# A mixer and two MLPs in split float32: x laid out twice, parameters as columns, TensorE's loops written out

## The reference

```python
u = rms_norm(h, mix_pre_gain)
p = u @ w_in                                     # 2048 x 5120
b_gate, c_gate, v_a, val_b, gate_b = split(p)
y_a = b_gate * causal_dwconv(c_gate * v_a, conv_a_w)          # 3 taps
g = causal_dwconv(val_b * sigmoid(gate_b), conv_b_w) + conv_b_bias   # 31 taps
y_b = silu(layer_norm(g, ln_b_gain, ln_b_bias))
h = h + rms_norm(concat(y_a, y_b) @ w_out, mix_post_gain)
m = rms_norm(h, mlp_pre_gain)
z = square(relu(m @ w_up)) @ w_down              # 2048 x 8192 and back
h = h + rms_norm(z, mlp_post_gain)
```

```python
proj = rmsnorm(h, g_mix) @ w_in_2                # q, k, v and three gates
merged = sum(sigmoid(gate_b) * (o_b @ w_branch_b) for b in range(3))
h = h + merged @ w_out_2
h = h + (silu(f @ w_gate) * (f @ w_up)) @ w_down_2   # f = rmsnorm(h, g_ffn)
```

## Time and profile before

| | us |
|---|---|
| median of 3 runs (2528.92 to 2530.01) | 2529.46 |
| the profiled execution's own time | 2525.66 |
| its span, first to last instruction | 2523.9 |

### The profile page before, as it was taken

The page is one execution under the profiler, slowest core; times in us unless marked ns, Lnnn a source line. Parts: engine busy times, 40 slices in busy tenths (PEclk is TensorE's granted clock), DMA queues, the critical chain, the costliest instruction groups (busy, mean ns, idle before and its releaser), DMA issues.

```text
span 2523.9 us, 30348 instructions
## 1 busy us (share of the span) xinstructions
PE 2489.8 (99%) x11139; PEld 2064.8 (82%) x11139; DVE 1455.9 (58%) x1552; ACT 1361.6 (54%) x1721; POOL 67.0 (3%) x78
## 2 busy tenths in 40 slices
PE   8999999999999999899999999999999999999999
PEld 7888878888788788788888888888888888888887
DVE  5888566555455455665566645545555555555554
ACT  5886566456455455454475544445555445544453
POOL 0110000000000000010100000000000000000000
PEclk9999999999999999999999999999999999999999
DMA  7897668677667676455555566665667666766665
GB/s 248 240 264 213 201 174 234 209 214 217 197 184 218 183 212 205 150 191 186 184 181 168 173 195 189 190 194 171 198 203 209 203 194 200 206 206 195 202 192 167
DMA packets 304214, 502.40 MB, mean 199 GB/s; under 512 B 70276, under 2 KB 70844, under 8 KB 303836
## 3 DMA queue, kind: packets, MB, share of 16 engines
q1 hardware_dynamic: 299372, 483.78, 62.9%
q0 software_dynamic: 4688, 16.93, 3.1%
q10 hardware_dynamic: 32, 0.01, 0.0%
HBM read 474.42 MB, written 4.47 MB: 190 GB/s over the span
## 4 chain that ended last, share of the span: by engine, by line
PE 98%; ACT 1%; DVE 1%; issue 0%; DMA 0%; POOL 0%; SPq 0%; ACTq 0%; DVEq 0%
PE acc L429 32%; PE acc L431 32%; PE acc L430 32%; PE tp L446 1%; PE po L615 0%; DVE w_lo L1074 0%; ACT w_hi L696 0%; PE sc L585 0%; DMA h<-x_dram 0%; ACT yb L846 0%; PE tp L603 0%; PE po L617 0%; ACT ev L703 0%; PE sc L446 0%; PE po L446 0%
## 5 line engine op out<-in xcount | busy, mean ns | idle before, releaser
L1074 DVE TENSOR_TENSOR w_lo<-raw,w_hi 128x1024 fp32r<-128x1024 f32 x888 | 1077.3, 1224 | 887.5 <-ACT w_hi L696 886.7
L696 ACT ACTIVATE w_hi<-raw 128x1024 fp32r<-128x1024 f32 x888 | 931.8, 1059 | 960.2 <-PE acc L431 933.7
L429 PE MATMUL acc<-w_lo,a_hi 128*128 128x512 f32 x2304 | 902.7, 392 | 9.8 <-issue 8.6
L431 PE MATMUL acc<-w_hi,a_lo 128*128 128x512 f32 x2304 | 898.0, 390 | 0.0
L430 PE MATMUL acc<-w_hi,a_hi 128*128 128x512 f32 x2304 | 897.7, 390 | 0.0
L430 PEld LDWEIGHTS acc<-w_hi,a_hi 128*128 128x128 f32 x2304 | 433.7, 188 | 96.0 <-issue 7.3
L429 PEld LDWEIGHTS acc<-w_lo,a_hi 128*128 128x128 f32 x2304 | 433.7, 188 | 92.9 <-issue 3.7
L431 PEld LDWEIGHTS acc<-w_hi,a_lo 128*128 128x128 f32 x2304 | 433.4, 188 | 90.6
L429 PE MATMUL acc<-w_lo,b_hi 128*128 128x512 f32 x1120 | 436.2, 389 | 0.3 <-DVE w_lo L1074 0.3
L431 PE MATMUL acc<-w_hi,b_lo 128*128 128x512 f32 x1120 | 435.7, 389 | 0.0
L430 PE MATMUL acc<-w_hi,b_hi 128*128 128x512 f32 x1120 | 435.7, 389 | 0.0
(11 more groups left out here) (171 smaller groups left out, 949.0 us busy)
## 6 DMA issues: line engine op xcount, KB each, us to landing
raw<-w_in_dram SPq DMA_DIRECT2D x272, 512.0 KB, 4.5
raw<-w_down_dram SPq DMA_DIRECT2D x216, 512.0 KB, 4.7
raw<-w_gu_dram SPq DMA_DIRECT2D x176, 512.0 KB, 4.4
raw<-w_up_dram SPq DMA_DIRECT2D x128, 512.0 KB, 3.9
raw<-w_out_dram SPq DMA_DIRECT2D x64, 512.0 KB, 4.6
raw<-w_branch_dram SPq DMA_DIRECT2D x32, 512.0 KB, 3.7
tap_sum<-tap_add POOLq DMA_DIRECT2D x20, 512.0 KB, 7.0
skew_dram<-line_dram POOLq DMA_DIRECT2D x12, 192.0 KB, 4.8
```

Of the source, the lines that this page charges most:

```text
L429: nc.tensor.matmul(out, xh, wl, start=s == 0 and k == 0, stop=False)
L431: mm = nc.tensor.matmul(out, xl, wh, start=False, stop=s == n - 1 and k == KS - 1)
L696: nc.scalar.activation(w_hi[:, ring], raw[:, ring], ACT.Copy).then_inc(hi_ready, 1)
L1074: nc.vector.tensor_tensor(w_lo[:, ring], raw[:, ring], w_hi[:, ring].bitcast(F32), ALU.subtract).then_inc(lo_ready, 1)
```

## The change

- The caller's program lays out two more inputs: `xT`, x with channels on partitions (128 x 16 x 256), and `cols`, all parameters per channel as columns (128 x 384). Both are made from the inputs by reordering alone.
- The first unit takes its activations from `xt`, loaded in eight pieces of two channel blocks (256 KB each), one behind each weight slot. ScalarE makes `a_hi` and VectorE `a_lo` from it directly, slot by slot. TensorE has no transposes in unit 0 and none of parameters; the product of the bias table moves behind unit 1.
- The rows of x are still needed, for the sums of squares and the residual. They are loaded in unit 1, one quarter behind each of its first four slots; ScalarE takes the squares while it prepares those slots.
- The other parameters, the tables and the identity are loaded behind unit 1's slots.
- TensorE's three loops become Python loops, so that its program has their bodies in full: 10785 rows of instructions for 8064. The loops of the other engines stay.

```diff
@@ -64,7 +63,7 @@
 G_FF3 = G_FF + 192
 G_DN3 = G_FF3 + 48
 G_END = G_DN3 + 24
-T_X, T_IN, T_N1, T_N2, T_QK, T_ATT, T_M, T_N3, T_FF = 0, 8, 20, 28, 36, 52, 68, 76, 84
+T_IN, T_N1, T_N2, T_QK, T_ATT, T_M, T_N3, T_FF = 0, 12, 20, 28, 44, 60, 68, 76
 S_X, S_YA, S_YB, S_N1, S_MLP, S_N2, S_O, S_M, S_N3, S_FF = 0, 8, 12, 16, 24, 56, 64, 80, 88, 96
 K_QK, K_ATT = 8, 24
 X_MLP, X_FF = 0, 16
@@ -100,7 +99,7 @@
         a_lo = at("a_lo", 64, [P, KT, S], F32R)
         b_hi = at("b_hi", 80, [P, KT, S], F32R)
         b_lo = at("b_lo", 96, [P, KT, S], F32R)
-        rows = at("rows", 112, [P, 4, P])
+        xt = at("xt", 80, [P, KT, S])
         onehot = at("onehot", 114, [32, LINE])
         lmask = at("lmask", 116, [H_SOFT, LINE])
         line = at("line", 118, [H_SOFT, LINE])
@@ -307,32 +307,28 @@
                     ).then_inc(planes_turned, 16)
-            sp.dma_start(ident[:, :], t["ident"]).then_inc(ident_in, 16)
-            for c in range(NCH):
-                sp.dma_start(h[:, :, c], x_v[:, :, c]).then_inc(x_in[c], 16)
-                load(c, None, w_in[:, ks(c), IN_COLS[0]:IN_COLS[0] + W])
-
-            small = ((16, "mlp_pre_gain", KT), (32, "g_mix_2", KT), (48, "g_ffn_2", KT),
-                     (64, "conv_b_bias", CT), (72, "ln_b_gain", CT), (80, "ln_b_bias", CT),
-                     (88, "conv_a_w", K_A * CT))
-            for r0, name, n in small:
-                src = t[name][0]
-                src = (src.rearrange("(c p) -> c p", p=P) if len(src.shape) == 1
-                       else src.rearrange("k (c p) -> (k c) p", p=P))
-                sp.dma_start(rows[r0:r0 + n, 0, :], src).then_inc(rows_in, 16)
-            taps = t["conv_b_w"][0].rearrange("k (c p) -> (k c) p", p=P)
-            for i in range(2):
-                sp.dma_start(rows[0:124, 1 + i, :], taps[124 * i:124 * (i + 1), :]).then_inc(rows_in, 16)
-            sp.dma_start(rows[0:H_SOFT, 3, :], t["q_gain_2"][0]).then_inc(rows_in, 16)
-            sp.dma_start(rows[H_SOFT:2 * H_SOFT, 3, :], t["k_gain_2"][0]).then_inc(rows_in, 16)
-            sp.dma_start(onehot[:, :], t["onehot"]).then_inc(line_in, 16)
-            sp.dma_start(lmask[:, :], t["lmask"]).then_inc(line_in, 16)
-            sp.dma_start(relb[:, :], t["rel_bias_2"]).then_inc(line_in, 16)
+            def load_xt(s):
+                sp.dma_start(xt[:, ks(s), :], t["xT"][:, ks(s), :]).then_inc(xt_in[s], 16)
+
+            for s in range(RING):
+                load(s, None, w_in[:, ks(s), IN_COLS[0]:IN_COLS[0] + W])
+                load_xt(s)
             for u in range(10):
                 for s in range(SPU):
                     g = G_IN + u * SPU + s
-                    if g >= RING:
-                        load(g, g, w_in[:, ks(s), IN_COLS[u]:IN_COLS[u] + W])
+                    if g < RING:
+                        continue
+                    if u == 0:
+                        load_xt(s)
+                    load(g, g, w_in[:, ks(s), IN_COLS[u]:IN_COLS[u] + W])
+                    if u == 1 and s < NCH:
+                        sp.dma_start(h[:, :, s], x_v[:, :, s]).then_inc(x_in[s], 16)
+                if u == 1:
+                    sp.dma_start(onehot[:, :], t["onehot"]).then_inc(line_in, 16)
+                    sp.dma_start(lmask[:, :], t["lmask"]).then_inc(line_in, 16)
+                    sp.dma_start(relb[:, :], t["rel_bias_2"]).then_inc(line_in, 16)
+                    sp.dma_start(cols[:, KT:3 * P], t["cols"][:, KT:3 * P]).then_inc(cols_in, 16)
+                    sp.dma_start(ident[:, :], t["ident"]).then_inc(ident_in, 16)
             with sp.Fori(0, NCH // 2) as j:
                 src = w_out[:, :, bass.ds(sp.snap(j * (2 * W)), 2 * W)]
@@ -458,24 +454,13 @@
                         slots(g, u, 2 * c - 2, 2 * c, a_hi, a_lo, split0=split0)
-            pe.wait_ge(ident_in, 16)
-            pe.wait_ge(pre_in, 16)
-            nc.tensor.transpose(sc[:, 0:KT], rows[0:KT, 0, :], ident[0:KT, 0:KT]).then_inc(cols_T, 1)
-            pe.wait_ge(cols_ok, 1)
-            turn_residual(G_IN, 0, [(x_in[c], 16) for c in range(NCH)], S_X)
-            slots(G_IN, 0, SPU - 2, SPU, a_hi, a_lo, split0=S_X)
-
-            pe.wait_ge(rows_in, 16 * 11)
-            pe.wait_ge(cols_ok, 1)
-            start = 0
-            for i, n in enumerate(ROWS):
-                tr = nc.tensor.transpose(sc[:, start:start + n], rows[0:n, i, :], ident[0:n, 0:n])
-                start += n
-            tr.then_inc(cols_T, 1)
+            slots(G_IN, 0, 0, SPU, a_hi, a_lo, split0=S_X)
+            slots(G_IN + SPU, 1, 0, SPU, a_hi, a_lo, pair=1)
             pe.wait_ge(line_in, 48)
             nc.tensor.matmul(po[0:H_SOFT, 0:LINE], relb[:, :], onehot[:, :], start=True,
-                             stop=True).then_inc(cols_T, 1)
+                             stop=True).then_inc(line_mm, 1)
+            pe.wait_ge(ident_in, 16)
             def in_product(u):
@@ -488,7 +473,7 @@
                     turn(ev[:, u % 2 ^ 1], (evacuated, u), (took, 7) if u == 9 else (ya, 1))
-            for u in range(1, 9):
+            for u in range(2, 9):
                 slots(G_IN + u * SPU, u, 0, 3, a_hi, a_lo, pair=u % 2)
                 in_product(u)
                 slots(G_IN + u * SPU, u, 3, SPU, a_hi, a_lo, pair=u % 2)
@@ -551,13 +536,13 @@
                     slots(gj, u + (NCH + j), 0, SPU, b_hi, b_lo, split0=split0, pair=j % 2)
             mlp_block(0, True)
-            with pe.Fori(1, FF1 // D) as b:
+            for b in range(1, FF1 // D):
                 mlp_block(b, False)
             turn_residual(G_QK, U_QK, [(h_ready, NCH + c + 1) for c in range(NCH)], S_N2)
             pe.wait_ge(split_lo, S_N2 + SPU)
-            with pe.Fori(0, NCH) as i:
+            for i in range(NCH):
                 for p_ in range(2):
                     g, u = G_QK + i * (2 * SPU) + p_ * SPU, U_QK + i * 2 + p_
                     slots(g, u, SPU - 2, SPU, a_hi, a_lo, pair=p_)
@@ -635,7 +620,7 @@
             pe.wait_ge(split_lo, S_O + NH)
             branches(G_B0, U_B0, 0, U_B0 % 2)
-            with pe.Fori(1, NCH) as j:
+            for j in range(1, NCH):
                 g, u = G_J - 4 * SPU + j * (4 * SPU), U_J - 6 + j * 6
                 for b in range(3):
                     slots(g + b * SPU, u + b, 0, 2, a_hi, a_lo, pair=b % 2)
@@ -746,19 +731,29 @@
                     nc.scalar.activation(junk[:, tk], src[:, tk], ACT.Square,
                                          accum_out=ssq[:, n, tk, c:c + 1]).then_inc(squared, 1)
-            pre = t["mix_pre_gain"][0].rearrange("(c p) -> c p", p=P)
-            act.dma_start(rows[0:KT, 0, :], pre).then_inc(pre_in, 16)
+            act.dma_start(cols[:, 0:KT], t["cols"][:, 0:KT]).then_inc(pre_in, 16)
             act.wait_ge(const_set, 1)
             nc.scalar.activation(den[:, :], half[:, :], ACT.Copy)
-            act.wait_ge(cols_ok, 1)
-            for c in range(NCH):
-                split(T_X + 2 * c, a_hi, 4 * c, G_MIXPRE, turn_banks[c % 2])
-                ticks(G_IN, 2 * c, 2 * c + 2)
-            for c in range(NCH):
-                squares(0, c, h[:, :, c], 2 * c)
+            act.wait_ge(pre_in, 16)
+
+            def xt_hi(s):
+
+                act.wait_ge(xt_in[s], 16)
+                for kt in (KS * s, KS * s + 1):
+                    a_ = nc.scalar.activation(a_hi[:, kt, :], xt[:, kt, :], ACT.Copy,
+                                              scale=cols[:, G_MIXPRE + kt:G_MIXPRE + kt + 1])
+                a_.then_inc(split_hi, 1)
+
+            for s in range(SPU):
+                if s < RING:
+                    ticks(G_IN, s, s + 1)
+                    xt_hi(s)
+                else:
+                    xt_hi(s)
+                    ticks(G_IN, s, s + 1)
             def scale_taps():
@@ -806,9 +801,16 @@
                                          ACT.Copy).then_inc(took, 1)
             for u in range(10):
-                if u < 2:
-                    ticks(G_IN + u * SPU, RING if u else SPU, RING + SPU)
+                if u == 0:
+                    for c in range(NCH):
+                        ticks(G_IN, SPU + c, SPU + c + 1)
+                        act.wait_ge(x_in[c], 16)
+                        squares(0, c, h[:, :, c], 2 * c)
                     evacuate_in(u)
+                elif u == 1:
+                    ticks(G_IN + SPU, RING, RING + SPU)
+                    evacuate_in(u)
+                    act.wait_ge(cols_in, 16)
                 elif u < 9:
                     for s in range(SPU):
                         ticks(G_IN + u * SPU, RING + s, RING + s + 1)
@@ -1122,15 +1124,24 @@
             nc.vector.memset(qkg[:, :], 1.0).then_inc(step0, 1)
-            dve.wait_ge(cols_T, 1)
-            nc.vector.tensor_copy(cols[:, 0:KT], sc[:, 0:KT]).then_inc(cols_ok, 1)
-            dve.wait_ge(cols_ok, 1)
-
-
-            for c in range(NCH):
-                split(S_X + 2 * c, a_hi, a_lo, 4 * c, G_MIXPRE, turn_banks[c % 2])
-                ticks(G_IN, 2 * c, 2 * c + 2)
```

(49 more changed lines are left out.)

## The result

The changed kernel takes 2511.06 us (median of 5 runs, 2510.59 to 2512.55), the kernel before 2529.46 beside it (5 runs, 2526.99 to 2531.31): ratio 0.9927, 95% interval 0.9916 to 0.9938. The profiled execution of the changed kernel took 2510.78 (span 2508.7) against 2525.66 of before: 14.9 less, where the sum said 13.5; that is 1.4 of the 4.9. The other 3.5 are the distance between a median and its profiled execution: 3.8 before, 0.3 now.

The account below looks back on a forecast made before the run. TensorE, busy for 99% of the span, was taken as the bound. Loop edges 10.5 us and start 3.0 took 13.5 off 2525.66, giving 2512.2; with 3.8 to the median, 2516.0, 8-in-10 range 2512.5 to 2520.

Parts of the forecast that it names:

- the sum: Whole kernel: loop edges 10.5 us plus start 3.0, 13.5 us off the profiled execution of 2525.66.
- Distance of profile and median: Whole kernel: the median stays 3.8 us above the profiled execution, with about 0.7 allowed for it.
- the low clock: TensorE at 1.2 GHz against 2.4: 2.4 us lost to it after the new start, 1.6 more than before.
- The loop of L554: TensorE's two jumps back there: stops and low clock cost 10.5 us, all gained by writing the loop out.
- The stop is the jump, not a wait for data: At L554's edges: TensorE's stop comes from the branch itself, which took 4.15 and 4.45 us.
- The rule of 2048 instructions: Skill's figure: L554's body, 1536 instructions, would be resident, its jump free, gain 0; set aside for the trace.
- The five short jumps: Jumps back of L560 and L638: costed at 0, at most 1.2 us gained.
- The start: Up to unit 0's end: 2.4 - 1.6 + 2.2 = 3.0 us earlier, first product at 9.0; bounds 1.1 to 4.1.
- Start worth nothing: Rival at the start: first transfers land late and the clock stays low long; 2519.0 us, chance 0.08.
- Cover at the edge fails: Rival at L554's edges: ScalarE becomes the wait, 5 of the 10.5 us return; 2521 us, chance 0.07.
- the stop stays in straight code: Rival at L554's edges: the stop isn't the jump, only the start's gain is left; 2526.5 us, chance 0.05.
- A starved queue: Rival in units 0 and 1: below 230 GB/s TensorE pauses at each slot; slower, 2551 us, chance 0.03.

Follow-up runs that it names:

- e12: The kernel before, unchanged, profiled a third time as a single execution: 2532.64 us.
- e2: The kernel before with L554 alone written out, start and other loops as before: 2516.15 us, ratio 0.995.
- e3: The changed kernel with the loop of L554 as a loop again, new start and short loops written out kept: 2511.47 us, ratio 0.993.
- e5: The kernel before with 24 small products (96 instructions) added at the very start of TensorE's list: 2521.23 us, ratio 0.9969.
- e6: e3 with 24 small products (96 instructions) added at the start: 2515.01 us, ratio 0.9942.
- e9: e3 with 12 small products (48 instructions) added at the start: 2512.66 us, ratio 0.9934.
- e13: e3 with 4, 16 or 19 small products added in TensorE's wait ahead of the first residual: 2512.74, 2517.45 and 2523.12 us.
- e4: The changed kernel with the two short loops (queries and keys; gates and branches) as loops again: 2511.58 us, ratio 0.993.
- e8: The changed kernel with 20 transposes on TensorE ahead of the first product, identity loaded early for them: 2509.95 us, ratio 0.9921.
- e11: The changed kernel with the rows of x loaded at the start, one quarter behind each of the first four slots: 2512.35 us, ratio 0.9927.
- shift 48: L554's body with 48 more TensorE instructions ahead of it than in e3, as in e9: 2512.66 us.
- shift 79: L554's body with 79 more TensorE instructions ahead of it than in e3, as in the kernel before: 2529.46 us.
- e7: The changed kernel with 13 float32 products of 128 columns on TensorE ahead of the first product: 2508.70 us, ratio 0.9916.

## Why the prediction was right, and where it was wrong

**Distance of profile and median: the step that failed.** "The median of the runs shown, 2529.46, is 3.8 above that execution; I take this distance to stay." It fell to 0.3, and that is 3.5 of the 4.9 us; the other 1.4 are the start, below. The distance was no property of runs in general: it was for the most part the jumps, which cost 10.5 us in the execution that I read and 14.6 in e12's, and to a lesser part the low clock at the start and the residual. Removing the jumps removed it (e2: all five runs within 1.1 us, its profiled one 0.8 above the median). In medians the change gave 18.4 us, 13.3 for the jumps (e2) and 5.1 for the start (e2 to after), where the sum had 10.5 and 3.0 and kept the rest as a constant. The width that I gave the distance, 0.7, was far too narrow: with no distance at all the same bounds of start and loops reach down to 2509.9.

**The loop of L554.** Between the first profiles the two edges gave 10.5 us as worked out, with no idle, no low clock and ScalarE in time: right. By medians e2 makes it 13.3. Wrong is what the step credits: in the changed kernel the loop could have stayed (e3), since the new start had already moved its body to a free place. The two parts of the change aren't additive: writing the loop out is worth 13.3 on top of the old start and 0.4, within the noise, on top of the new one. "The stop is the jump, not a wait for data" holds for before; that such a jump stops TensorE was true for one place of the body only.

**The rule of 2048 instructions.** I set the Trainium skill's figure ("Runtime: NRT & Kernel Launch", Instruction fetch mechanics) aside by the earlier trace rows. For before the rows were right. But e3 shows a body of this length (1618 rows of the trace, not the 1536 that I counted) that is kept and jumps for free, as that figure says it should. What decides, by e3, e5 and e6 against before, e9 and e13, is whether it covers 7 blocks or, because it begins near a block's end, 8. Why 8 blocks of some 250 rows, about the room of that figure, are not kept is open. My error was to read one place of the body as a property of its length.

**The five short jumps.** Costed at 0, and 0 they are (e4).

**The start.** Between the profiles it gave about 4.8 us where I had 3.0 (bounds 1.1 to 4.1). The first product is at 8.12, not 9.0: the first slot landed at 4.80, 4.05 us after its issue, and I had taken the 4.89 of x's transfer, and VectorE's pieces followed at once. That is 0.9 of the 1.8. The low clock lost 1.66, not 2.4, which is most of the rest, and this part is luck: other executions of the same start lost 2.4 to 2.9, and the old start's 0.8 was from a cheap execution too (e8). The choice of 2.4 was sound; taking both losses from a single profile each was not. Units 0 and 1 ran without a pause, so no queue starved; with the rows loaded early there are pauses (e11), so the later loading does something. The whole start by medians: e2 to after, 5.1 us.

**The rivals.** Start worth nothing: refuted by e2 against after. Cover at the edge fails, or the stop stays in straight code: refuted by the windows of 14.00. A starved queue: refuted, TensorE is busy for 20.00 of 20 us with the queue at 371 GB/s.

## What to carry to other kernels

Before a sum is set against a median, look at several runs: here a spread of 6 us, where the kernels whose jumps are free or gone spread by 3 or less, meant that a stop has a varying price, and one profile showed its cheap end. Whether a long loop's jump is free depends on where the body lies, which any edit ahead of it can change; so compare the branch's own duration in the new kernel before crediting an edit with it, and write out a loop only where that duration says so. Where TensorE idles before dense work, cheap products that end just in time are worth the low clock's loss: 4.3 us in three places here. But look at the steps of the next products in the new trace: 10.4 us of e6's small products didn't bring the clock up.

## What the runs showed of the hardware

- The branch of the same body takes 0.21 to 0.24 us or 3.8 to 4.7, by the place of the body; what TensorE loses at each jump ahead of its next product runs from 0 through 0.4 to 0.5 us (shift 48) to 3.0 to 5.8 (shift 79, three profiles).
- Adding 96 small instructions to before made it 8.3 us faster (e5).
- A float32 product is two matmul instructions here: 24 products left 48 rows of matmul in 10.42 us, 0.217 us each for 16 columns.
- Ahead of the first product, 4.7 us of float32 products of 128 columns (e7) or 4.1 us of transposes (e8) brought the full clock; 10.4 us of float32 products of 16 columns (e6) left the next products at twice the step.
- What remains open: why the second fetch costs more in one execution than in another of the same kernel (the pause behind the first weight load is 4.27 and 3.00 us in the first profile of before, 4.14 and 4.67 in e12's), and why the clock's first rise comes at 11.47 in after and 13.41 in e3 with the same start. No run tells either apart.
